# Prologue of a two-layer encoder: scale tiles on VectorE alone, another order of loads, rotary tables later

## The reference

```
c_act = silu(c)
for l in range(2):
    mod = c_act @ w_ada[l] + b_ada[l]          # six vectors of 1024
    shift_a, scale_a, gate_a, shift_f, scale_f, gate_f = split(mod, 6)
    h = rms_norm(x, g_attn) * (1 + scale_a) + shift_a
    proj = h @ w_in                             # q, k, v, latents
    ... attention of both groups, output projection ...
    x = x + gate_a * o
    h = rms_norm(x, g_ffn) * (1 + scale_f) + shift_f
    u = conv3(h @ w_up); x = x + gate_f * ((silu(gate) * val) @ w_down)
return rms_norm(x, g_final)
```

## Time and profile before

| | us |
|---|---|
| time before, median of 3 runs (lowest, highest) | 1219.42 (1215.99, 1219.92) |
| the profiled execution | 1219.4 |
| its span | 1217.6 |
| TensorE busy | 1177.2 (97%) |
| VectorE, ScalarE, GpSimd busy | 729.2, 543.0, 566.2 |
| mean granted TensorE clock | 0.984 of full |

### The profile page before, as it was taken

How to read it: one execution, slowest core, us unless ns; L and a number is a source line. 1 busy time by engine, 2 the same in 40 slices (tenths; PEclk the granted TensorE clock), 3 DMA queues, 4 the chain that set the end, 5 groups by cost and what they waited for, 6 DMA issues and landing times.

```text
span 1217.6 us, 18912 instructions
## 1 busy us (share of the span) xinstructions
PE 1177.2 (97%) x6356; PEld 1017.0 (84%) x6356; DVE 729.2 (60%) x1479; ACT 543.0 (45%) x888; POOL 566.2 (47%) x774
## 2 busy tenths in 40 slices
PE   9999998999999999999899999899999999999997
PEld 8897887898888888888789888879988888888886
DVE  4777878776767677767566376446676134412446
ACT  4347675345432344234354577734443133423442
POOL 2487400644655545645565450044454645554462
PEclk6999899999999999999999999999999999999999
DMA  9743322323446345544423222022242323232322
GB/s 357 286 155 140 100 91 88 114 95 121 155 152 210 122 173 172 190 147 165 144 97 113 86 97 70 1 70 87 86 164 96 104 87 103 90 100 87 104 87 70
DMA packets 43691, 151.55 MB, mean 124 GB/s; under 512 B 4962, under 2 KB 7522, under 8 KB 43620
## 3 DMA queue, kind: packets, MB, share of 16 engines
q1 hardware_dynamic: 43620, 150.64, 36.1%
HBM read 148.52 MB, written 2.10 MB: 124 GB/s over the span
## 4 chain that ended last, share of the span: by engine, by line
issue 34%; PE 33%; POOL 21%; POOLq 8%; DVE 2%; DMA 1%; DVEq 0%; SPq 0%; ACT 0%; ACTq 0%
POOL w_lo L527 19%; PE ps L607 10%; PE ps L608 10%; PE ps L613 10%; POOLq L528 7%; DMA ada_raw<-ada_slots 1%; PE ps L711 1%; POOL qb_tmp L574 1%; DVE ada_prod L1542 1%; POOL qb L579 1%; POOLq L585 1%; POOL kb L582 0%; PE ps L719 0%; PE ps L733 0%; DVE x L1474 0%
## 5 line engine op out<-in xcount | busy, mean ns | idle before, releaser
L527 POOL TENSOR_TENSOR w_lo<-w_raw,w_hi 128x256 fp32r<-128x256 f32 x712 | 529.6, 775 | 626.0 <-ACT w_hi L1078 604.3
L607 PE MATMUL ps<-h_hi,w_hi 128*128 128x512 f32 (+1 forms) x960 | 349.1, 364 | 6.0 <-DVEq L1495 4.0
L608 PE MATMUL ps<-h_lo,w_hi 128*128 128x512 f32 (+1 forms) x960 | 346.3, 361 | 0.0
L613 PE MATMUL ps<-h_hi,w_lo 128*128 128x512 f32 (+1 forms) x960 | 346.3, 361 | 0.0
L1078 ACT CAST w_hi<-w_raw 128x1024 fp32r<-128x1024 f32 x178 | 182.9, 1047 | 192.2 <-PE ps L607 190.3
L607 PEld LDWEIGHTS ps<-h_hi,w_hi 128*128 128x128 f32 x960 | 181.1, 189 | 39.6 <-DVEq L1495 5.4
L1737 DVE SCALAR_TENSOR_TENSOR u_sb<-ps,par,u_sb 128x510 f32<-128x510 f32 x176 | 131.8, 749 | 129.2 <-ACT u_sb L1291 116.6
L613 PEld LDWEIGHTS ps<-h_hi,w_lo 128*128 128x128 f32 x960 | 181.2, 189 | 27.5
L608 PEld LDWEIGHTS ps<-h_lo,w_hi 128*128 128x128 f32 x960 | 181.2, 189 | 26.8
L607 PE MATMUL ps<-a_hi,w_hi 128*128 128x512 f32 (+1 forms) x400 | 147.1, 368 | 6.3 <-DVEq L1529 6.3
L608 PE MATMUL ps<-a_lo,w_hi 128*128 128x512 f32 (+1 forms) x400 | 146.0, 365 | 0.0
(11 more groups left out here) (145 smaller groups left out, 1433.1 us busy)
## 6 DMA issues: line engine op xcount, KB each, us to landing
w_raw<-w_slots SPq DMA_DIRECT2D x178, 512.0 KB, 3.5
ada_raw<-ada_slots SPq DMA_DIRECT2D x88, 512.0 KB, 3.9
shift<-shift_slots SPq DMA_DIRECT2D x8, 512.0 KB, 14.3
x_tok<-x_rows SPq DMA_DIRECT2D x4, 512.0 KB, 6.6
x<-x_t SPq DMA_DIRECT2D x4, 512.0 KB, 13.0
y_t<-x SPq DMA_DIRECT2D x3, 512.0 KB, 2.9
y_t<-x SPq DMA_DIRECT2D x1, 256.0 KB, 2.9
y_t<-x SPq DMA_DIRECT2D x2, 128.0 KB, 2.7
```

Of the source, the lines that this page charges most:

```text
L527: nc.gpsimd.tensor_tensor(w_lo[:, j, c], w_raw[:, j, c], w_hi[:, j, c].bitcast(F32), ALU.subtract)
L607: hh = mm(out, stat[0], mov[0], start=first, stop=False)
L608: hl = mm(out, stat[0], mov[1], start=False, stop=False)
L613: return mm(out, stat[1], mov[0], start=False, stop=last)
```

## The change

Scale tile 0 moves from TensorE to VectorE, shift tile 7 from TensorE to VectorE (its weights are laid out for that on the host). The loads come in another order, and of the parameters the 43 columns that the prologue needs come first, by themselves. The keep-warm matmuls stand elsewhere. ScalarE's square of the token rows, first shift tiles and cast of slot 0 are interleaved anew, and the casts of slots 1, 2, 3 stand behind k = 1, 3, 5. GpSimd makes the rotary tables behind w_lo of slot 3. The core of the diff:

```
+SHIFTS_DVE = 1
+PC_FIRST = PC_BADA + 2 * KD
@@ SyncE: loads, in order
             sp.dma_start(ident[:], ident_d).then_inc(ident_landed, 16)
+            load_ada(0, 0)
+            sp.dma_start(par[:, 0, 0:PC_FIRST], params[:, 0, 0:PC_FIRST]).then_inc(par_first_landed, 16)
+            load_shift(0)
+            load_ada(0, 1)
             load_rows(0)
+            load_slot(0)
             load_rows(1)
-            load_ada(0, 1)
+            load_ada(0, 2)
+            load_shift(1)
             load_rows(2)
             load_rows(3)
-            load_shift(0)
-            load_ada(0, 0)
-            sp.dma_start(par[:], params).then_inc(par_landed, 16)
-            load_slot(0)
-            load_ada(0, 2)
             load_x(0)
-            load_shift(1)
+            load_ada(0, 3)
+            load_shift(2)
+            load_slot(1)
             load_x(1)
...
+            load_ada(0, 4); load_shift(3); load_slot(2); load_ada(0, 5); load_shift(4); load_x(2)
+            load_ada(0, 6); load_shift(5); load_slot(3); load_ada(0, 7); load_shift(6)
             (gqk, tab)
-            sp.wait_ge(shift_full, 1)
...
+            load_x(3); load_shift(7)
+            sp.dma_start(par[:, 0, PC_FIRST:], params[:, 0, PC_FIRST:]).then_inc(par_landed, 16)
+            sp.dma_start(par[:, 1, :], params[:, 1, :]).then_inc(par_landed, 16)
@@ GpSimd
-                    for n in range(2):
+                    for n in range(RING):
                         lo_slot(n, n)
                     head_tables(0)
-                    for n in range(2, RING):
-                        lo_slot(n, n)
@@ TensorE
-            for t in range(1, TT):
-                pe.wait_ge(rows_landed[t], 16)
-                keep_warm(6)
@@ shift_tile(j)
-                if j < SCALES_PE:
-                    pe.wait_ge(ada_landed[j], 16)
-                    (eight matmuls of scale tile j)
@@
                     shift_tile(0)
+                    keep_warm(16, 5)
+                    shift_tile(1)
+                    pe.wait_ge(c_rows_ready, NSEQ)
+                    keep_warm(10, 0)
                     for s in range(NSEQ):
                         norm_roots(0, s)
-                    shift_tile(1)
-                    pe.wait_ge(c_rows_ready, NSEQ)
+                    keep_warm(4, 0)
@@
-                        if k + 2 < KD:
+                        if k + 2 < KD - SHIFTS_DVE:
                             shift_tile(k + 2)
@@ ScalarE
+            prepare(ACT.Sqrt)
+            square_rows(0)
+            act.wait_ge(par_first_landed, 16)
+            take_shift(0)
             split_hi(0, 0)
-            act.wait_ge(par_landed, 16)
-            act.wait_ge(scale1_ready, 1)
-            take_shift(0)
+            for t in range(1, TT):
+                square_rows(t)
+            A(root[:], st_o[:, 0, 0:TT], ACT.Sqrt, bias=eps[:], scale=1.0 / D_MODEL).then_inc(root_ready, 2)
+            take_shift(1)
             for k in range(KD):
                 (h_hi of k)
-                if k + 1 < KD:
+                if 2 <= k + 1 < KD - SHIFTS_DVE:
                     take_shift(k + 1)
-                if k in (0, 2, 4):
+                if k in (1, 3, 5):
                     split_hi(0, 1 + k // 2)
                 if k == 6:
                     split_hi(0, 4)
+            act.wait_ge(par_landed, 32)
@@ VectorE
+            scale_sum(0, 0)
+            scale_sum(1, 0)
+            scale_sum(0, 1)
+            scale_sum(1, 1)
+            dve.wait_ge(par_first_landed, 16)
+            (scale1; scale_end of 0 and 1; sums and end of 2; root_inverse)
@@ loop over k
-                if k < SCALES_PE:
-                    dve.wait_ge(shift_done, k + 1)
                 (xn of k)
-                if 1 <= k < KD - SCALES_PE - 1:
-                    scale_tile(k + SCALES_PE + 1)
+                if 1 <= k < KD - 2:
+                    for s in range(NSEQ):
+                        scale_sum(k + 2, s)
+                    scale_end(k + 2)
+                if k == KD - 2:
+                    shift_on_vector(KD - 1)
                 (h_lo of k)
+            dve.wait_ge(par_landed, 32)
@@ new on VectorE
+            def shift_on_vector(k):
+                dve.wait_ge(shift0_landed[k], 16)
+                for s in range(NSEQ):
+                    V.scalar_tensor_tensor(out=ada_prod[:], in0=shift0[:, k, :], scalar=1.0, in1=c_all[:, s, :],
+                                           op0=ALU.mult, op1=ALU.mult, accum_out=part[:, 1, k, s:s + 1])
+                    V.drain()
+                V.tensor_scalar(mod[:, 0, SHIFT_A, k, :], part[:, 1, k, :],
+                                par[:, 0, PC_BADA + SHIFT_A * KD + k:PC_BADA + SHIFT_A * KD + k + 1], None, ALU.add)
+                V.drain()
```

More of the change, by code:

```diff
@@ L127 @@
 ADA_RING = 4
-SCALES_PE = 1
+SHIFTS_DVE = 1
+PC_FIRST = PC_BADA + 2 * KD
 HALVED = (4, 5, 6, 7, 8, 10)
@@ L347, in encoder_kernel @@
         shift_done = sem("shift_done")
+        par_first_landed = sem("par_first_landed")
         par_landed = sem("par_landed")
@@ L706, in down_tile, with keep_warm @@
                     last.then_inc(full[bank(key)], 1)
-            def keep_warm(n):
+            def keep_warm(n, b):
                 for _ in range(n):
-                    mm(ps[:, 5, P:2 * P], ones[:], ones[:], start=True, stop=True)
+                    mm(ps[:, b, P:2 * P], ones[:], ones[:], start=True, stop=True)
             pe.wait_ge(const_ready, 1)
-            keep_warm(8)
+            keep_warm(8, 5)
             pe.wait_ge(ident_landed, 16)
@@ L734, in shift_tile @@
                               stop=(k == KD - 1))
-                if j < SCALES_PE:
-                    pe.wait_ge(ada_landed[j], 16)
-                    for k in range(KD):
-                        last = mm(ps[:, 4 + j % 2, NSEQ:2 * NSEQ], ada_raw[:, j, k * P:k * P + P], cact[:, k, :],
-                                  start=(k == 0), stop=(k == KD - 1))
                 last.then_inc(shift_full, 1)
@@ L1104, in _, with square_rows @@
             act.wait_ge(const_ready, 1)
[L1105 to L1109, removed]
+            for s in range(NSEQ):
+                act.wait_ge(rows_full, s + 1)
+                nc.scalar.copy(c_all[:, s, :].rearrange("p (b c) -> p b c", b=2), ps[:, 2 * s:2 * s + 2, :]
+                               ).then_inc(c_rows_ready, 1)
+            prepare(ACT.Sqrt)
+            def square_rows(t):
                 act.wait_ge(rows_landed[t], 16)
@@ L1112, in _ @@
                 nc.scalar.drain()
-            A(root[:], st_o[:, 0, 0:TT], ACT.Sqrt, bias=eps[:], scale=1.0 / D_MODEL).then_inc(root_ready, 2)
             def take_shift(j):
@@ L1119, in take_shift @@
                   bias=par[:, 0, PC_BADA + SHIFT_A * KD + j:PC_BADA + SHIFT_A * KD + j + 1])
-                if j < SCALES_PE:
-                    A(mod[:, 0, SCALE_A, j, :], ps[:, 4 + j % 2, NSEQ:2 * NSEQ], ACT.Identity,
-                      scale=par[:, 0, PC_GATTN + j:PC_GATTN + j + 1], bias=scale1_g[:, j:j + 1])
                 nc.scalar.drain()
                 act.sem_inc(shift_done, 1)
+            square_rows(0)
+            act.wait_ge(par_first_landed, 16)
+            take_shift(0)
             split_hi(0, 0)
-            act.wait_ge(par_landed, 16)
-            act.wait_ge(scale1_ready, 1)
-            take_shift(0)
+            for t in range(1, TT):
+                square_rows(t)
+            A(root[:], st_o[:, 0, 0:TT], ACT.Sqrt, bias=eps[:], scale=1.0 / D_MODEL).then_inc(root_ready, 2)
+            take_shift(1)
             for k in range(KD):
@@ L1532, in update_x, with scale_sum @@
                     dve.sem_inc(x_upd, 1)
[L1535 to L1545, removed]
+            dve.sem_inc(ada_used, 4)
+            def scale_sum(k, s):
+                if s == 0:
+                    dve.wait_ge(ada_landed[k % 4], 16 * (k // 4 + 1))
+                if k == 0:
+                    dve.wait_ge(c_rows_ready, s + 1)
+                V.scalar_tensor_tensor(out=ada_prod[:], in0=ada_raw[:, k % 4, :], scalar=1.0, in1=c_all[:, s, :],
+                                       op0=ALU.mult, op1=ALU.mult, accum_out=part[:, 0, k, s:s + 1])
+                V.drain()
+                if s == NSEQ - 1:
+                    dve.sem_inc(ada_used, 1)
             def scale_end(k):
@@ L1550, in scale_end @@
                 V.drain()
-            def scale_tile(k):
-                scale_sums(k)
+            def shift_on_vector(k):
[6 more added lines that the diff above has]
+                                par[:, 0, PC_BADA + SHIFT_A * KD + k:PC_BADA + SHIFT_A * KD + k + 1], None, ALU.add)
+                V.drain()
+            scale_sum(0, 0)
[3 more added lines that the diff above has]
+            dve.wait_ge(par_first_landed, 16)
+            V.tensor_scalar(scale1[:], par[:, 0, PC_BADA + SCALE_A * KD:PC_BADA + (SCALE_A + 1) * KD], 1.0, None, ALU.add)
+            V.drain()
+            for k in range(2):
                 scale_end(k)
-            scale_sums(SCALES_PE)
```

(7 more changed lines are left out.)

27 lines of the change are left out of this document (11 added, 16 removed).

## The result

| | before | changed |
|---|---|---|
| median of 6 runs each, us | 1219.60 (1215.99 to 1220.05) | 1225.17 (1223.45 to 1228.97) |
| ratio of the changed to the one before | | 1.0041, interval 1.0028 to 1.0055 |
| the same, measured again with the experiments | 1220.62 (33 runs) | 1224.84 (10 runs), ratio 1.0035, 1.0024 to 1.0046 |
| profiled execution, its span | 1219.4, 1217.6 | 1226.7, 1224.9 |

The account below looks back on a forecast made before the run. VectorE and TensorE were taken as nearly even ahead of layer 0's second projection chunk, with TensorE busy nearly all the time afterwards. 1219.4 + 2.3 (second chunk later) + 0.6 (clock) = 1222.3 us, range 1215.5 to 1228.

Parts of the forecast that it names:

- The step that decides: Layer 0's projection: casts one step later make k = 2, 4, 6 wait for w_lo, 4.7 us beside two sums.
- The lock rule: VectorE instructions with two SBUF inputs and GpSimd ones reading SBUF exclude each other entirely; w_lo would be 5.3 us.
- the give-back: In the projection steps, a late shift tile lets VectorE's sums finish before w_lo starts, taking back about 1.5 us.
- The start: Prologue: first product of layer 0's projection at 24.6 against 25.24, a gain of 0.6 us; bounds 23.5 and 26.
- Rival D: Slower start: shift tiles among keep-warm matmuls leave the clock low; start 1.4 later, k = 0 slower by 2.8; 1226.5; chance 0.08.
- The gain of k = 0: First projection step at 2.4 GHz takes 4.55 us with its shift tile instead of 7.4, a gain of 2.8 us.
- Tables: Rotary tables between w_lo of slots 3 and 4: 4.0 us; w_lo of slot 4 ends at 65.8, second chunk 2.3 later.
- Clock: TensorE's waits ahead of k = 2 and k = 4 may bring clock falls; 0.6 us added in all.
- rival C: Slower: clock falls ahead of k = 2, k = 4 and the second chunk; 8.2 us, 1227.6; chance 0.21.
- One for one: A shift of the second chunk's start in layer 0's projection carries unchanged to the end of the kernel.
- mechanism A: The forecast itself: w_lo waits, late tables and clock make it slower; 1222.3 us, spanning 1219.5 to 1225; chance 0.46.

Follow-up runs that it names:

- the third execution: The changed kernel, nothing altered, run and traced a third time; 1223.4 us in one execution, against one of 1221.4 of the kernel before.
- the second execution: The changed kernel, nothing altered, run again beside variants of it; ratio to the kernel before 1.0035 (1.0024 to 1.0046).
- the order before: Kernel before, unchanged or with four or nine keep-warm matmuls ahead of layer 0's second chunk, or late rotary tables; ratios of these three 1.0001, 1.0018, 1.0003.

## Why the prediction was right, point by point

- **The step that decides** was named rightly and sized well. w_lo beside the sums took 4.34, 4.17 and 4.16 us against the 4.7 used; TensorE waited for it ahead of k = 2, 4 and 6 in all three executions of the changed kernel; the steps came at 36.08, 46.71 and 57.33 against 35.8, 47.0 and 58. That they agree so closely is in part luck: the start was 0.7 us late, and each pair of steps took 10.6 to 10.8 us and not 11.2. The cast experiments show it as a cause: early casts remove the waits and bring 2.6 to 3.3 us by ratios of different rounds, late casts alone make waits of 2.1 us and cost 1.8 us by a ratio whose interval includes no change.
- **The lock rule** of the Trainium skill (SBUF — State Buffer, Who interferes with whom) would have given 5.3 us for w_lo. The measured 4.2 to 4.4 beside sums is under both 4.7 and 5.3; w_lo here met only the end of the first sum and, behind the second, h_lo, which took 1.72 us instead of 0.88. Where TensorE's low clock made the shift tile late, w_lo started behind the sums and took 3.15 (slot 2 of the third execution), and the wait ahead of k = 4 was 0.36: the give-back that the clock's term counted on.
- **The start**: 25.30 in the profiled execution against 24.6, and 28.3 in another. Forecast as a gain of 0.6 us, it was a loss of 1.7 on average. This is the step that failed in size: TensorE's line up to norm_roots was taken from one execution, with L719 at 4.3 us. With this L719 the sum is 0.7 short, 0.4 of it in shift tile 0 and the keep-warm matmuls behind it, and 0.2 in xn and h_lo (1.7 and not 1.5); with the long one it is 3.7 short. Rival D put a loss in the right place, but by a low clock at k = 0; k = 0 ran at full clock in all three executions. Fewer keep-warm matmuls are worth 0.27%, though the traces show only 0.5 us of that at the start.
- **The gain of k = 0** (2.8 us) came: 25.30 to 29.84 is 4.54 us, by the same step as forecast. With shift tile 7 gone from TensorE (1.7 us) it paid for most of the 6.0 us of waits in the steps, not for all of them and a later start.
- **Tables**: 3.1 us, not 4.0, and w_lo of slot 4 2.82, not 3.2. It ended at 63.66, 0.9 us ahead of TensorE, which had lost 1.7 us to its low clock in k = 6 and 7: there the term was hidden behind the clock. In the second execution it was likewise 1.1 us ahead; in the third TensorE did wait for slot 4, 0.66 us, and with few keep-warm matmuls 0.54. So the term was on the path or within about 1 us of it, and not the 2.2 us between k = 7 and slot 4 that the sum has.
- **Clock** (0.6 us, and rival C): too small, about 2.1 on average. The three executions of the changed kernel had falls in the projection's stretch at 58.8; at 51.1 and 61.3; at 35.0 and 48.7, with 3.4, 6.8 and 10.2 us at half clock; the four of the order before had 3.4, 0, 3.4 and 3.4. C's mechanism took part of the loss, without its three falls in each execution. By the Trainium skill (TensorE: Matmul & The Clock Gate, HAM oscillation) waits between short bursts bring the slow clock back; the falls at or just behind the waits for w_lo agree, but only five of the nine such waits had one.
- **One for one** holds on average, to about 1 us, and not for a pair: the profiled pair gave 1.0 us at the second chunk and 7.3 us in all.

So the forecast of 2.9 us was right in its sign and in its mechanism and short by 1.4 to 2.1 us by the two ratios, from the start and the clock. The sum has luck in it too: it had the steps from first product to second chunk at 41.2 us, and they took 39.9, which hides most of the 1.7 us by which the start was later than the 24.6 forecast. The measured 1225.17 lies just above what the forecast's own mechanism A was given (1219.5 to 1225).

## What to carry to other kernels

When an order by hand is changed, count for each producer how long ahead of its use it now stands: one step less of lead for a cast was a wait in every second step. A wait that goes may uncover the next one close behind it: with w_lo off the path, h_lo held TensorE. Keep-warm matmuls are work on TensorE's queue; put them only where it would wait anyway, and see what stands behind them in the worst state of the clock, not in the one that the trace shows. Differences of a few us in a long kernel need several traces, since half-clock stretches far from the change moved single executions by more than the change itself.

## What the runs showed of the hardware

The low-clock stretches of one and the same kernel lie elsewhere in each execution, as the three traces of the changed one show. The single executions of the kernel before spread over 6.4 us (1216.9 to 1223.4), and L719 alone took 3.8 to 4.3 us in ten traces and 7.2 in four. In these four L719, and in the three of the new order shift tile 0 behind it (3.57 us), ran at the pace of the low level while the granted clock reads 1.00, so the column alone doesn't tell the pace at the start. VectorE's instructions of two SBUF inputs and GpSimd's subtraction stretch each other: in the changed kernel the sum went from 1.23 to 1.59 us, h_lo from 0.88 to 1.72, and w_lo from 2.82 to 4.34. A GpSimd instruction of the tables beside no sum took 0.46 us where it took 1.02 beside a sum before.
